# A two-layer encoder on one core: the opening's gate product, the order behind it, and the first strip of an up projection

## The chip, the core and the metric

The kernel runs on one core of a Trainium2 chip. The metric is the device time of one execution in microseconds (us), the median of three runs. The core has a matrix engine (TensorE, PE in the rows; its weight loads are PEld), a vector engine (VectorE, DVE), ScalarE (ACT), GpSimd (POOL) and SyncE (SP), which run side by side and wait for one another on semaphores. Matrix products go to eight banks of PSUM, 512 float32 wide; everything else lies in SBUF.

## The reference

The input is 1024 tokens of 1024 numbers. Layer 0 mixes them with 8 stick-breaking and 8 forgetting heads of 64, layer 1 with 16 heads over a shared latent and a top-k choice of keys; each layer ends in a gated feed-forward block of width 2816 with a causal convolution. What matters here, cut from it:

```python
h = x @ w_in                                   # layer 0: q, k, v of 16 heads, and 8 gate columns
f_logit = parts[6] + b_f
cum = jnp.cumsum(jax.nn.log_sigmoid(f_logit.astype(F32)), axis=1)
logits = (q @ k) * scale + cq[..., None] - cum_k[:, :, None, :]     # forgetting heads
w = exp(log_sigmoid(z) + after)                # stick-breaking heads
x = layer_norm(ALPHA * x + mixer(x))
gate, up = jnp.split(x @ w_up, 2, axis=-1)
x = layer_norm(ALPHA * x + (gelu(conv(gate)) * up) @ w_down)
```

## The kernel before

**Numbers in two parts.** Every float32 operand is split into a high and a low bfloat16 part (`_hi`, `_lo`), and a product is three matmuls: high by high, high by low, low by high. A weight piece of 128x1024 is loaded by SP into one of four slots (`w_stage`), its high part is made by POOL or ScalarE (`w_hi`), its low part by POOL (`w_lo`), and a slot is free again when TensorE has used it (`w_used`).

**The opening** (`start_*`). The transposed input `xt_f` comes in eight tiles `k`; for each, ScalarE makes `xt_hi` and the vector engine `xt_lo`, and TensorE runs the gate product (8 columns of weights, both halves of the tokens, into banks 0 and 1: line 475) and two halves of pair 0's projection of q (`proj_half`, line 573). Then ScalarE computes the log-sigmoid of the gate in four steps (lines 431 to 437), the vector engine scans it into a cumulative sum (`gate_c`, line 501) and writes it as three bfloat16 parts into `cum_rows` (lines 504 to 507, three rounds). The forgetting heads alone need these, and they come after the four stick-breaking pairs.

**The heads** (`heads_*`). TensorE goes on with halves 2 to 5 of pair 0's projection (k, then v: lines 573 and 579). ScalarE copies each half out of PSUM as a high part (`proj_evac_hi`, line 619), the vector engine the low part (`proj_evac_lo`, line 624), and ScalarE issues the DMAs that lay q and k (`make_current_qk`, six for each head of the pair, line 636) and v (`make_current_v`, two each, line 644) as the scores need them, and three that store `cum_rows` (line 1041). Then `all_pairs` runs eight pairs of heads, 16 slots each: a slot has the scores of one block of queries on TensorE (lines 745 and 748), for stick-breaking two sigmoids on ScalarE (`stay`, `take`, lines 832 and 834), a scan on the vector engine (line 881) and a product on POOL (line 902). The next pair's projection is run in between, into bank 4; `half_slots` says which part in which slot. `heads_gpsimd` splits the pieces of the next pair (lines 890 and 895), each when its use in the projection is over.

**The end of a mixer** (`back_and_norm`, tags `o0` and `o1`; the same function, with 22 tiles in place of 8, ends the feed-forward blocks). The output projection runs in two groups of four blocks of 128 tokens, the late half of the tokens first (line 317). The vector engine adds the residual and normalizes; TensorE turns a normalized block with eight transposes (`turn`, line 1204); ScalarE writes its high parts and a float32 copy (`highs`, lines 1258 and 1260) and the vector engine its low parts (`lows`, line 1332). In between TensorE runs the first products of the up projection: `unit(n, h, ks)`, strip `n` over token half `h`, by `early_strips` and `product_part` (line 341), late half first. On ScalarE the order is written by hand: `deviation(i)` is the root of block i's variance, `piece_hi` the high part of a strip. On each engine the order of the code is the order of execution; an instruction that waits holds up all behind it on its engine.

## Time and profile before

| | |
|---|---|
| median of three runs | 2903.4 us (2902.46 to 2911.68) |
| the profiled execution | 2908.67 us, its span 2906.9 us |
| TensorE busy | 2803.3 us, 96% of the span |
| vector engine, POOL, ScalarE busy | 64%, 57%, 37% |
| mean granted clock of TensorE | 0.991 |

A row of a timeline is: start in us, duration in us, engine, line, operation, output<-inputs, how many; and in square brackets how long the engine stood idle before it, with what ended that. Matmuls overlap: the next starts before the row of the last is over. Lines with ACTq or SPq are the issuing of DMAs. The granted clock is the share of TensorE's full clock (2.4 GHz) that it was given in a stretch; it has two levels, full and half.

### The profile page before, as it was taken

What the parts mean: (1) busy time and instruction counts of PE and PEld (TensorE: products, weight loads), DVE (VectorE), ACT (ScalarE), POOL (GpSimd) and SP (SyncE); (2) the same over time, 40 slices, a digit from 0 to 9 for tenths busy, and PEclk for the clock granted to TensorE, in tenths of its full rate; (3) what the DMA queues carried; (4) which work ended last, traced back from release to release, by engine and by line L of the source; (5) the groups of instructions that cost most, each with busy time, mean ns of one, the idle gap of its engine ahead of it and who ended that gap; (6) DMA issues with size and microseconds to landing.
All of it is one profiled execution on the core that took longest, in us unless ns stands there. A gap on an engine that the chain in (4) does not pass through costs nothing.

```text
span 2906.9 us, 44833 instructions
## 1 busy us (share of the span) xinstructions
PE 2803.3 (96%) x16880; PEld 1457.2 (50%) x16880; DVE 1872.9 (64%) x2732; ACT 1081.6 (37%) x1765; POOL 1651.6 (57%) x915
## 2 busy tenths in 40 slices
PE   7999998899999999999899999999999999999998
PEld 3566665444444444444444444677764444444443
DVE  5787666475666664355999999677756656665042
ACT  3565555333333310013553333666653333332000
POOL 3677545426666669845348777500013466665884
PEclk9999999999999999999999999999999999999999
DMA  4122222431111144222213222211113211113322
GB/s 146 48 62 67 61 67 47 157 119 44 59 59 59 59 158 145 102 81 77 59 37 145 101 88 85 74 59 43 58 71 111 80 59 58 59 59 111 135 102 102
DMA packets 102990, 240.57 MB, mean 83 GB/s; under 512 B 42448, under 2 KB 42576, under 8 KB 102848
## 3 DMA queue, kind: packets, MB, share of 16 engines
q1 hardware_dynamic: 56352, 204.13, 19.6%
q10 hardware_dynamic: 46496, 34.48, 4.6%
q8 instruction: 97, 1.59, 0.2%
q14 instruction: 45, 0.37, 0.0%
HBM read 185.31 MB, written 31.51 MB: 75 GB/s over the span
## 4 chain that ended last, share of the span: by engine, by line
PE 86%; DVE 5%; ACT 3%; issue 2%; ACTq 1%; POOL 1%; DMA 0%; POOLq 0%; DVEq 0%
PE ps L1483 22%; PE ps L317 19%; PE ps L306 14%; PE ps L2290 6%; PE ps L573 5%; PE ps L341 4%; PE ps L2326 2%; PE ps L683 2%; PE ps L579 2%; PE ps L1810 2%; PE ps L768 2%; PE ps L745 2%; PE ps L1854 1%; PE ps L2305 1%; DVE pt_lo L704 1%
## 5 line engine op out<-in xcount | busy, mean ns | idle before, releaser
L262 POOL TENSOR_TENSOR w_hi<-w_stage,ones 128x1024 bf16<-128x1024 f32 (+1 forms) x115 | 235.0, 2044 | 138.1 <-PE ps L317 85.1
L265 POOL TENSOR_TENSOR w_lo<-w_stage,w_hi 128x1024 bf16<-128x1024 f32 (+1 forms) x115 | 262.7, 2284 | 9.0
L1300 DVE SCALAR_TENSOR_TENSOR x_res<-x_res,ps 128x1024 f32<-128x1024 f32 x32 | 39.0, 1218 | 338.4 <-PE ps L317 337.5
L317 PE MATMUL ps<-w_hi,hid_hi 128*128 128x512 bf16 x704 | 209.4, 379 | 0.8 <-POOL w_lo L265 0.8
L317 PE MATMUL ps<-w_lo,hid_hi 128*128 128x512 bf16 x704 | 209.4, 379 | 0.0
L317 PE MATMUL ps<-w_hi,hid_lo 128*128 128x512 bf16 x704 | 209.4, 379 | 0.0
L2290 PE MATMUL ps<-lat_hi,q_now 128*128 128x512 bf16 (+3 forms) x768 | 197.7, 326 | 0.0
L306 PE MATMUL ps<-xt_hi,w_hi 128*128 128x512 bf16 x608 | 181.8, 381 | 2.5 <-DVE score L1969 2.5
L306 PE MATMUL ps<-xt_hi,w_lo 128*128 128x512 bf16 x608 | 181.3, 380 | 0.0
L306 PE MATMUL ps<-xt_lo,w_hi 128*128 128x512 bf16 x608 | 181.3, 380 | 0.0
L279 POOL TENSOR_TENSOR w_lo<-w_stage,w_hi 128x1024 bf16<-128x1024 f32 x32 | 76.6, 2399 | 155.4 <-ACT w_hi L272 155.2
L1483 PE MATMUL ps<-xt_hi,w_hi 128*128 128x512 bf16 x432 | 163.7, 379 | 0.0
L1483 PE MATMUL ps<-xt_lo,w_hi 128*128 128x512 bf16 x432 | 163.7, 379 | 0.0
L1483 PE MATMUL ps<-xt_hi,w_lo 128*128 128x512 bf16 x432 | 163.7, 379 | 0.0
L902 POOL TENSOR_TENSOR prob<-take,prob 128x1024 f32<-128x1024 f32 (+3 forms) x64 | 107.4, 1684 | 90.6 <-DVE prob L881 69.7
L2414 POOL COPY v_now_hi<-val_hi 128x512 bf16 (+1 forms) x16 | 9.8, 616 | 251.0 <-PE ps L2305 251.0
L1252 ACT ACTIVATE ln_rstd<-ln_rstd 128x1 f32<-128x1 f32 x32 | 6.5, 203 | 383.6 <-DVE ln_rstd L1312 383.5
L2205 DVE MATCH_REPLACE8 score<-best,score 128x512 f32<-128x512 f32 (+4 forms) x160 | 148.8, 943 | 0.0
L2202 DVE MAX8 best<-score 128x8 f32<-128x512 f32 (+4 forms) x160 | 140.5, 944 | 1.7
L1449 POOL TENSOR_TENSOR w_lo<-w_stage,w_hi 128x1024 bf16<-128x1024 f32 x36 | 76.7, 2130 | 113.5 <-ACT w_hi L1557 113.5
L2368 DVE CUSTOM_DVE_ANT_0 prob<-ps,hide 128x1024 f32<-128x1024 f32 (+7 forms) x128 | 96.5, 754 | 63.2 <-PE ps L2290 63.1
L704 DVE TENSOR_TENSOR pt_lo<-ps,pt_hi 128x512 bf16<-128x512 f32 x192 | 100.2, 549 | 51.7 <-ACT pt_hi L698 51.5
(293 smaller groups left out, 7896.9 us busy)
## 6 DMA issues: line engine op xcount, KB each, us to landing
w_stage<-in_l_up SPq DMA_DIRECT2D x88, 512.0 KB, 3.2
w_stage<-in_l_down SPq DMA_DIRECT2D x88, 512.0 KB, 3.2
w_stage<-in_l_o SPq DMA_DIRECT2D x32, 512.0 KB, 3.9
w_stage<-in_l_q SPq DMA_DIRECT2D x32, 512.0 KB, 4.8
q_split<-q_out SPq DMA_DIRECT2D x32, 512.0 KB, 2.6
q_now<-q_split SPq DMA_DIRECT2D x16, 1024.0 KB, 4.8
w_stage<-in_l_qkv SPq DMA_DIRECT2D x24, 512.0 KB, 3.3
x_spilled<-x_res ACTq DMA_DIRECT2D x16, 512.0 KB, 2.6
```

Source lines behind the costliest of these rows:

```text
L262: pool.tensor_tensor(w_hi[slot][:, 0:cols], w_stage[slot][:, 0:cols], ones[:, 0:1].to_broadcast([P, cols]), ALU.mult).then_inc(w_cast[slot ...
L265: pool.tensor_tensor(w_lo[slot][:, 0:cols], w_stage[slot][:, 0:cols], w_hi[slot][:, 0:cols], ALU.subtract).then_inc(w_split[slot], 1)
L306: mm = pe.matmul(ps[:, bank + h, :], w, a[:, k, h * HALF:(h + 1) * HALF], start=(first and k == k0 and m == 0), stop=(last and k == k1 - 1 ...
L317: mm = pe.matmul(ps[:, bank + h, :], a[:, k, rows], w[slot][:, h * HALF:(h + 1) * HALF], start=(k == 0 and m == 0), stop=(k == tiles - 1 a ...
L341: mm = pe.matmul(ps[:, bank + h, :], w, a[:, k, h * HALF:(h + 1) * HALF], start=(k == 0 and m == 0), stop=(k == KT - 1 and m == 2))
L573: mm = pe.matmul(ps[:, bank, :], w, a[:, u, h * HALF:(h + 1) * HALF], start=(u == 0 and m == 0), stop=(u == KT - 1 and m == 2))
L704: dve.tensor_tensor(lo, src, hi, ALU.subtract).then_inc(self.lo, 1)
L902: pool.tensor_tensor(prob[t % 4][:, 0:n], take[t % 4][:, 0:n], prob[t % 4][:, 0:n], ALU.mult).then_inc(s_wsb, 1)
L1483: mm = pe.matmul(ps[:, bank, :], wk[:, k * P:(k + 1) * P], ak[:, k, :], start=(k == 0 and q == 0), stop=(k == 3 and q == 2))
L2202: dve.max(best[:, c, :], cells[c]).then_inc(s_top, 1)
L2205: dve.match_replace(cells[c], best[:, c, :], cells[c], TAKEN_SCORE).then_inc(s_rep, 1)
L2290: mm = pe.matmul(ps[:, 2 * (t % 2) + c // 512, 0:w], a, b, start=(kt == 0 and m == 0), stop=(kt == 1 and m == 2))
```

## The change

It has four pieces. (1) The gate product: in place of three matmuls per half and `k` with 8 columns of weights there are two with 40 columns. `wf_both` holds the high part in columns 0 to 7 and the low part in columns 32 to 39, `wf_wide` the high part in columns 0 to 7 and zeros elsewhere. Rows 0 to 7 of PSUM then hold two of the three products and rows 32 to 39 the third; ScalarE takes rows 32 to 39 with the bias, and the vector engine adds rows 0 to 7 to them. (2) The order behind it, on the vector engine and ScalarE; the waits of TensorE for the gate and for all six halves of pair 0 go or become a wait for three. (3) In `back_and_norm` with eight tiles (`o0` and `o1`): ScalarE's `piece_hi` of strip 0 stands before `deviation(GROUP + 2)`. (4) There too: strip 0's unit over the early half is cut into 384 tokens, after the third block's low parts, and 128, after the fourth's.

```diff
-        def product_part(pe, feed, n, h, ks):
+        def product_part(pe, feed, n, h, ks, cols=slice(0, HALF)):
...
-                    mm = pe.matmul(ps[:, bank + h, :], w, a[:, k, h * HALF:(h + 1) * HALF],
+                    mm = pe.matmul(ps[:, bank + h, cols], w, a[:, k, h * HALF + cols.start:h * HALF + cols.stop],
...
-            act.activation(gate_x[:, :], banks(0)[0:8, :], ACT.Identity, bias=gate_b[:, 0:1]).then_inc(s_gact, 1)
-            act.wait_ge(s_gact, 1)
+            act.activation(gate_x[:, :], banks(0)[32:40, :], ACT.Identity, bias=gate_b[:, 0:1]).then_inc(s_gact, 1)
+            act.wait_ge(s_gdve, 1)
...
+            pool.memset(wf_both[:, :, :], 0.0).then_inc(s_wfh, 1)
+            pool.memset(wf_wide[:, :, :], 0.0).then_inc(s_wfh, 1)
+            pool.wait_ge(s_wfh, 2)
             pool.wait_ge(s_wf, 32)
-            pool.tensor_copy(wf_hi[:, :, :], wf_f[:, :, :]).then_inc(s_wfh, 1)
-            pool.wait_ge(s_wfh, 1)
-            pool.tensor_tensor(wf_lo[:, :, :], wf_f[:, :, :], wf_hi[:, :, :], ALU.subtract).then_inc(s_wfl, 1)
+            pool.tensor_copy(wf_both[:, :, 0:8], wf_f[:, :, :]).then_inc(s_wfh, 1)
+            pool.tensor_copy(wf_wide[:, :, 0:8], wf_f[:, :, :]).then_inc(s_wfl, 1)
+            pool.wait_ge(s_wfh, 3)
+            pool.tensor_tensor(wf_both[:, :, 32:40], wf_f[:, :, :], wf_both[:, :, 0:8], ALU.subtract).then_inc(s_wfl, 1)
...
-                    for m, (w, a) in enumerate(((wf_hi, xt_hi), (wf_hi, xt_lo), (wf_lo, xt_hi))):
-                        mm = pe.matmul(ps[0:8, h, :], w[:, k, :], a[:, k, h * HALF:(h + 1) * HALF],
+                    for m, (w, a) in enumerate(((wf_both, xt_hi), (wf_wide, xt_lo))):
+                        mm = pe.matmul(ps[0:40, h, :], w[:, k, :], a[:, k, h * HALF:(h + 1) * HALF],
...
+            gthen(dve.tensor_tensor(gate_x[:, :], banks(0)[0:8, :], gate_x[:, :], ALU.add))
...
-                    if not first:
+                    if isinstance(pair, int) and pair == 1 and e == 0:
+                        pe.wait_ge(s_pjl, 3)
+                    elif not first:
                         pe.wait_ge(s_pjl, 6 * pair + e)
...
+                if prev is None and slot == 8:
+                    act.wait_ge(s_gdve, GATE_STEPS)
+                    for r in range(3):
+                        act.dma_start(cum_dram[:, r, :], cum_rows[32 * r:32 * r + 8, :]).then_inc(s_cum, 16)
...
-            pe.wait_ge(s_gdve, GATE_STEPS)
...
-                pe.wait_ge(s_nl, 2 * TB * at + 2 * TB)
-                for n in range(4):
+                if tiles == KT:
+                    pe.wait_ge(s_nl, 2 * TB * at + 2 * (TB - 1))
+                    early(pe, 0, 0, range(KT), slice(0, HALF - P))
+                    pe.wait_ge(s_nl, 2 * TB * at + 2 * TB)
+                    early(pe, 0, 0, range(KT), slice(HALF - P, HALF))
+                else:
+                    pe.wait_ge(s_nl, 2 * TB * at + 2 * TB)
+                    unit(0, 0, range(KT))
+                for n in range(1, 4):
                     unit(n, 0, range(KT))
...
+                if tiles == KT:
+                    piece_hi(act, next_feed, 0)
                 deviation(GROUP + 2)
                 highs(3)
                 if tiles == KT:
-                    for n in range(SLOTS):
+                    for n in range(1, SLOTS):
```

What it does to the order is best seen engine by engine. The vector engine behind the opening's last `xt_lo`, before (`gate_*` is the gate, `nq`, `nk`, `nv` the parts of the projected pair):

```order
L499 TENSOR_SCALAR gate_m<-gate_x 8x1024
L501 SCALAR_TENSOR_TENSOR gate_c<-gate_m,gate_a 8x1024
L504 CAST gate_p<-gate_c 8x1024
L505 COPY cum_rows<-gate_p 8x1024
L507 TENSOR_TENSOR gate_c<-gate_c,gate_p 8x1024
L504 CAST gate_p<-gate_c 8x1024
L505 COPY cum_rows<-gate_p 8x1024
L507 TENSOR_TENSOR gate_c<-gate_c,gate_p 8x1024
L504 CAST gate_p<-gate_c 8x1024
L505 COPY cum_rows<-gate_p 8x1024
L624 TENSOR_TENSOR nq_lo<-ps,nq_hi 128x512 x2
L624 TENSOR_TENSOR nk_lo<-ps,nk_hi 128x512 x2
```

The same place in the changed kernel:

```order
L504 TENSOR_TENSOR gate_x<-ps,gate_x 8x1024
L505 TENSOR_SCALAR gate_m<-gate_x 8x1024
L507 SCALAR_TENSOR_TENSOR gate_c<-gate_m,gate_a 8x1024
L635 TENSOR_TENSOR nq_lo<-ps,nq_hi 128x512 x2
L512 CAST gate_p<-gate_c 8x1024
L513 COPY cum_rows<-gate_p 8x1024
L515 TENSOR_TENSOR gate_c<-gate_c,gate_p 8x1024
L635 TENSOR_TENSOR nk_lo<-ps,nk_hi 128x512
L512 CAST gate_p<-gate_c 8x1024
L513 COPY cum_rows<-gate_p 8x1024
L515 TENSOR_TENSOR gate_c<-gate_c,gate_p 8x1024
L635 TENSOR_TENSOR nk_lo<-ps,nk_hi 128x512
```

One addition is new at the front, the low parts of q and k stand between the gate's rounds, and the third round comes behind them. ScalarE from pair 0's last k half to its first score, before (the DMAs make the operands of the scores and store the gate):

```order
L619 ACTIVATE nk_hi<-ps 128x512 x2
L636 DMA q_both_101<-nq_hi 64x1024
L636 DMA q_both_101<-nq_lo 64x1024
L636 DMA k_twice_103<-nk_hi 64x1024 x2
L636 DMA q_ext_105<-nq_hi 64x1024
L636 DMA k_ext_107<-nk_lo 64x1024
L636 DMA q_both_102<-nq_hi 64x1024
L636 DMA q_both_102<-nq_lo 64x1024
L636 DMA k_twice_104<-nk_hi 64x1024 x2
L636 DMA q_ext_106<-nq_hi 64x1024
L636 DMA k_ext_108<-nk_lo 64x1024
L619 ACTIVATE nv_hi<-ps 128x512 x2
```

The same place in the changed kernel:

```order
L630 ACTIVATE nk_hi<-ps 128x512 x2
L647 DMA q_both_101<-nq_hi 64x1024
L647 DMA q_both_101<-nq_lo 64x1024
L647 DMA k_twice_103<-nk_hi 64x1024 x2
L647 DMA q_ext_105<-nq_hi 64x1024
L647 DMA k_ext_107<-nk_lo 64x1024
L630 ACTIVATE nv_hi<-ps 128x512 x2
L647 DMA q_both_102<-nq_hi 64x1024
L647 DMA q_both_102<-nq_lo 64x1024
L647 DMA k_twice_104<-nk_hi 64x1024 x2
L647 DMA q_ext_106<-nq_hi 64x1024
L647 DMA k_ext_108<-nk_lo 64x1024
```

The copies of v have moved ahead of the second head's six DMAs. In both kernels v's four DMAs follow; before, the three of `cum_rows` stood behind those and ahead of the first `stay`, and now they stand in slot 8. ScalarE in `o0`, around the third block of the late half being turned, before (`w_hi_66` to `w_hi_69` are the strips of the up projection in slots 0 to 3):

```order
L1263 DMA x_spilled<-x_res 128x1024
L1252 ACTIVATE ln_rstd<-ln_rstd 128x1
L1258 ACTIVATE xt_hi<-ps 128x4x128
L1260 ACTIVATE xt_f_130<-ps 128x4x128
L1258 ACTIVATE xt_hi<-ps 128x4x128
L1260 ACTIVATE xt_f_130<-ps 128x4x128
L1263 DMA x_spilled<-x_res 128x1024
L272 ACTIVATE w_hi_66<-w_stage_62 128x1024
L272 ACTIVATE w_hi_67<-w_stage_63 128x1024
L272 ACTIVATE w_hi_68<-w_stage_64 128x1024
L272 ACTIVATE w_hi_69<-w_stage_65 128x1024
```

The same place in the changed kernel:

```order
L1281 DMA x_spilled<-x_res 128x1024
L272 ACTIVATE w_hi_66<-w_stage_62 128x1024
L1270 ACTIVATE ln_rstd<-ln_rstd 128x1
L1276 ACTIVATE xt_hi<-ps 128x4x128
L1278 ACTIVATE xt_f_130<-ps 128x4x128
L1276 ACTIVATE xt_hi<-ps 128x4x128
L1278 ACTIVATE xt_f_130<-ps 128x4x128
L1281 DMA x_spilled<-x_res 128x1024
L272 ACTIVATE w_hi_67<-w_stage_63 128x1024
L272 ACTIVATE w_hi_68<-w_stage_64 128x1024
L272 ACTIVATE w_hi_69<-w_stage_65 128x1024
```

Strip 0's high part has moved ahead of a block's deviation and of its four copies.

## Rows read from the trace of the kernel before

**Rows 1.** Waits of TensorE in the whole span: us in total, times, longest us.

```profile
PE ps L683 <- DVE pt_lo L704: 35.2, 31, 2.5
...
PE ps L341 <- DVE xt_lo L1332: 7.9, 3, 3.0
PE ps L341 <- POOL w_lo L279: 7.4, 2, 3.7
```

**Rows 2.** Timeline of TensorE, the opening's first gate block.

```profile
9.48 0.63 PE L475 MATMUL ps<-xt_lo,wf_hi 128*8 128x512 bf16 x1
```

**Rows 3.** Timeline of POOL, 4 to 50 us.

```profile
4.96 0.24 POOL L462 CAST wf_hi<-wf_f 128x64 bf16<-128x64 f32 x1 [2.27 <-DMA gate_b<-in_l_bf]
...
47.43 2.46 POOL L895 TENSOR_TENSOR w_lo<-w_stage,w_hi 128x1024 bf16<-128x1024 f32 x1
```

**Rows 4.** Timeline of the vector engine, 37 to 50 us.

```profile
37.32 3.44 DVE L501 TENSOR_TENSOR_SCAN gate_c<-gate_m,gate_a 8x1024 f32<-8x1024 f32 x1 [2.66 <-ACT gate_a L437]
...
43.21 0.68 DVE L504 CAST gate_p<-gate_c 8x1024 bf16<-8x1024 f32 x1
...
47.92 2.24 DVE L505 COPY cum_rows<-gate_p 8x1024 bf16<-8x1024 bf16 x1
```

**Rows 5.** Timeline of ScalarE, from the gate to the first score.

```profile
32.84 1.11 ACT L431 ACTIVATE gate_x<-ps,gate_b 8x1024 f32<-8x1024 f32 x1 [13.91 <-PE ps L475]
...
52.77 0.54 ACTq L636 DMA_DIRECT2D q_both<-nq_hi  x1
...
60.51 1.09 ACT L619 ACTIVATE nv_hi<-ps 128x512 bf16<-128x512 f32 x2 [15.31 <-issue]
62.46 0.69 ACTq L644 DMA_DIRECT2D v_both<-nv_hi  x1
...
65.93 1.29 ACTq L1041 DMA_DIRECT2D cum_rows<-cum_rows  x3
67.26 1.02 ACT L832 ACTIVATE stay<-ps 128x1024 f32<-128x1024 f32 x1 [5.66 <-issue]
```

**Rows 6.** Timeline of TensorE, pair 0's first scores.

```profile
58.45 0.38 PE L745 MATMUL ps<-k_twice,q_both 128*128 128x512 bf16 x1 [3.16 <-DMA k_ext<-nk_lo]
```

**Rows 7.** Timeline of ScalarE, end of layer 0's mixer.

```profile
618.67 0.20 ACT L1252 ACTIVATE ln_rstd<-ln_rstd 128x1 f32<-128x1 f32 x1 [3.71 <-DVE ln_rstd L1312]
...
620.69 3.91 ACT L272 ACTIVATE w_hi<-w_stage 128x1024 bf16<-128x1024 f32 x4
```

**Rows 8.** Timeline of TensorE, end of layer 0's mixer.

```profile
608.09 1.06 PE L1204 MATMUL ps<-ident,x_res 128*128 128x128 f32 x8 [0.45 <-DVE xt_lo L1332]
...
624.94 0.38 PE L341 MATMUL ps<-xt_hi,w_hi 128*128 128x512 bf16 x1 [3.68 <-POOL w_lo L279]
...
653.95 0.61 PE L341 MATMUL ps<-xt_hi,w_hi 128*128 128x512 bf16 x1 [2.95 <-DVE xt_lo L1332]
```

**Rows 9.** Timeline of POOL, end of layer 0's mixer.

```profile
621.93 11.08 POOL L279 TENSOR_TENSOR w_lo<-w_stage,w_hi 128x1024 bf16<-128x1024 f32 x4 [21.96 <-ACT w_hi L272]
```

**Rows 10.** Timeline of the vector engine, end of layer 0's mixer.

```profile
620.92 0.69 DVE L1332 TENSOR_TENSOR xt_lo<-ps,xt_hi 128x512 bf16<-128x512 f32 x1 [0.28 <-ACT xt_f L1260]
...
649.54 1.28 DVE L1332 TENSOR_TENSOR xt_lo<-ps,xt_hi 128x512 bf16<-128x512 f32 x2
...
653.20 0.69 DVE L1332 TENSOR_TENSOR xt_lo<-ps,xt_hi 128x512 bf16<-128x512 f32 x1 [0.29 <-ACT xt_f L1260]
```

**Rows 11.** Stretches of TensorE: us, busy us (count), granted clock, DMA share, GB/s.

```profile
624.90:630.00 5.10, 5.06 (x16) 0.67 0.48 162
653.90:661.00 7.10, 7.05 (x19) 0.57 0.00 0
2278.50:2285.00 6.50, 6.45 (x24) 0.79 0.00 0
690.00:1060.00 370.00, 370.00 (x1716) 1.00 0.19 66
44.40:55.20 10.80, 10.80 (x193) 1.00 0.25 74
```

33 lines of the change are left out of this document (17 added, 16 removed).

## Prediction

> **What bounds the kernel now.** I read the waits of TensorE first, because the table above has it busy for 96% of the span: a change can only pay where TensorE stands still or runs slowly on the way. Two of the longer waits belong to the lines of this change: line 341 (the first units of an up projection) waits 7.4 us in two places for POOL's `w_lo`, and 7.9 us in three places for the vector engine's `xt_lo` [rows 1]. The third of these three is behind layer 0's down projection, where `tiles` is not `KT` and nothing changes. Then the opening's timelines, engine by engine, for the chain that leads to the first pair of heads. Last the stretches after the waits, for the granted clock, and 690 to 1060 us, where the up projection keeps TensorE busy without a gap at full clock [rows 11]: time won ahead of it can arrive there undiminished.
>
> **Part A, the opening.** *Matmuls.* A matmul of 512 columns takes 0.216 us of TensorE's time at full clock (370 us for 1716 of them [rows 11]; the 0.38 us of a row overlap). The change drops a third of the gate's 48 matmuls: two per `k`. From `k` = 1 on that is 7 x 2 x 0.216 = 3.0 us. The two of `k` = 0 ran at half rate (0.63 us in the row, overlapping again [rows 2]); what they save, 0.9 us at most, is partly spent in waiting for the first `w_lo`: I take 0.4. So the gate product ends at 29.4 instead of 32.8 us and the last projection of pair 0 at 51.8 instead of 55.2. POOL's two new memsets and one copy are costed at nothing: POOL waits 2.27 us for the gate's weights there, and its cast of them takes 0.24 us [rows 3], so that the memsets fit into the wait; uncovered, the three would cost under 1 us.
>
> *Gate chain.* ScalarE's `gate_x` starts at 32.84 [rows 5], now 29.45. The new addition on the vector engine (8x1024, two operands) has no row of its own; it is bounded by the cast (0.68 us) and by the scan (3.44) [rows 4]. I take 1.25, what the subtraction leaves of a gate round of 2.45 us, since it is the nearest in form. The scan then starts at 35.2 instead of 37.32 and ends at 38.6 at the latest. Then come two `nq_lo` (0.65 each: four such fill the time from 50.16, the copy's end, to 52.7), a round of cast, copy and subtraction (40.76 to 43.21: 2.45 us [rows 4]), and one `nk_lo`: 43.0. The next cast and copy fall on POOL's split of pair 1's second piece, which waits for the fourth projection half: its second step moves by 3.4 us from 47.43 to 44.0 [rows 3] and ends at about 46.1. Before, the copy beside that step needed 2.24 us [rows 4]; so it ends at about 46.3, the subtraction at 47.5, `nk_lo` at T1 = 48.1 us. Before, T1 was 52.7: the DMAs behind it start at 52.77 [rows 5].
>
> What the rows show: the copy that started at 47.92 ended 0.27 us behind POOL's step [rows 3, 4]. The Trainium skill, "SBUF — State Buffer", § Who interferes with whom, says that such a vector copy and a POOL operation lock each other out, and that whoever issues first keeps the ports for the whole instruction; the trace agrees. By that rule the copy could also come first, and T1 would be 45.5.
>
> *ScalarE to the first score.* Six DMAs take half of 7.74 us (52.77 to 60.51), 3.87; the four of `v` 3.47 (62.46 to 65.93); the `cum_rows` three 1.33 [rows 5]. Now: 48.1 + 3.87 = 52.0, two `nv_hi` 1.1 (TensorE is done at 51.8), six DMAs to 56.9, four to 60.4, and `stay` of slot 0 at 60.45 instead of 67.26: 6.8 us. With T1 = 45.5 TensorE's 51.8 binds and it is 7.4. TensorE itself started slot 0 1.9 us behind the sixth DMA issue (56.6), at 58.45 [rows 6], now at 54, and fits two projection parts in ahead of ScalarE. Removing its waits for the gate and for pair 0's `nv_lo` costs nothing and frees nothing more, since ScalarE then comes last. The `cum_rows` DMAs stand in ScalarE's slot 8 now: 1.33 us ahead of `stay`, with turned blocks queued behind it, whose `pt_hi` the vector engine and then TensorE wait for. Between nothing and 1.3 us I take 0.3, since TensorE has projections to run there. Part A: 6.5 us, with ends 4.5 and 7.5.
>
> **Part B, the first high part earlier (both layers).** ScalarE makes the four `w_hi` from 620.69 on; POOL starts the first `w_lo` 1.24 us later, at 621.93 (four in 11.08 us), and TensorE starts the unit at 624.94 [rows 7 to 9], having ended the output projection about 621.2 (the wait is 3.68). In the new order the first `w_hi` stands ahead of `deviation`, for which ScalarE waits until 618.67 [rows 7]. Its slot is free when TensorE has done the first of the last block's four products of six matmuls, 3 x 6 x 0.216 = 3.9 us before the end: 617.4. So `w_hi` runs from 617.4 to 618.5, still ahead of 618.67: the moved step is paid from idle time, and would cost 0.2 us for each 0.2 us that it came later. POOL starts at 618.7 and ends at 621.5 at the latest. Next late is `xt_lo` of the fourth block, 620.92 + 0.69 = 621.61 [rows 10], and TensorE starts at 621.67: 3.27 us sooner. The other three `w_lo` keep their times (621.9 on) and are 2 us ahead of TensorE's units of 5.2 us. The residue is a gap of 0.4 us; at 608.09 one of 0.45 us left no slow matmul behind it [rows 8].
>
> The clock comes on top. In 624.90 to 630.00 the mean grant is 0.67, 2.4 and 1.2 GHz mixed: (1 - 0.67) x 5.1 = 1.7 us are lost behind the wait of 3.68 us [rows 11]. Layer 1 has the same wait (two of 7.4 us together [rows 1]) and is taken alike. Part B: 2 x (3.27 + 1.7) = 9.9 us, 6.5 without the clock.
>
> **Part C, 384 tokens and then 128 (both layers).** TensorE stands 2.95 us before 653.95, until `xt_lo` of the last block (653.20 + 0.69) [rows 8, 10]. The first 384 tokens need only the block before: its two `xt_lo` end at 650.8 [rows 10], when TensorE ends the last turning (651.0). So the gap closes: 2.93 us. The 24 matmuls become 48. Of 128 columns, 193 took 10.80 us, 0.056 each, with their weight loads [rows 11]; 384 columns by interpolation to 0.216 are 0.163, an estimate. 24 x (0.163 + 0.056) = 5.25 against 24 x 0.216 = 5.18: 0.1 us more. The first part lasts 3.9 us, to 654.9, and the last block is ready at 653.9. Clock: (1 - 0.57) x 7.1 = 3.05 us in layer 0, (1 - 0.79) x 6.5 = 1.4 in layer 1 [rows 11]. Part C: 5.9 + 4.2 = 10.1 us, 5.7 without the clock. The up projection's next pieces are split once their slot's unit is done, so they move with TensorE; the token sums move with `xt_lo`, 6 us less, but TensorE reads them only two tile pairs (some 40 us) later.
>
> **Sum.** 6.5 + 9.9 + 10.1 = 26.5 us: the span goes from 2906.9 to 2880.4. The profiled execution lies 5.3 us above the median of the runs shown; against the median, 2903.4 - 26.5 = 2876.9.
>
> **Rivals.**
> 1. *The clock doesn't come back.* The engine stays slow for such stretches at these places, because turning and copying phases, not the two gaps, bring it down. Against: the slow stretches begin just behind the gaps. The gain is 26.5 - 7.8 = 18.7: 2884.7.
> 2. *The opening's gain is spent among the pairs.* TensorE waits 35.2 us in 31 places for `pt_lo` there [rows 1]; `cum_rows` at slot 8 and a slower first pair take it back: 20 us gained or somewhat less, 2883.
> 3. *Part B stays shut.* If the slot is released later than 617.4, or the `w_hi` delays `deviation` and the fourth block, each us of that takes a us, and the clock falls as before: without part B, 16.6 us, 2886.8.
> 4. *Slower.* The copy beside POOL took 2.24 us, 1.97 of it before POOL's step ended [rows 3, 4]. The four stick-breaking pairs have 64 scans, and a new phase between the vector engine and POOL could block more of them. From 14 more such waits on the path the 26.5 us are gone; 18 cost 35 us: 2912. Against: what starts the pairs moves as one, so the phase hardly changes.
> 5. *It doesn't do what it says.* If another semaphore held line 341 in both places, parts B and C give nothing: 2897. The waits' releasers speak against it.
>
> **How the numbers follow.** Forecast 0.66 (2872 to 2881), rival 1 0.10, rival 2 0.13, rival 3 0.06, rival 4 0.02, rival 5 0.03. The range goes down to 2869 (part A at 7.5, layer 1's clock loss at layer 0's size, 1.7 us more, and the scatter of the runs, some 5 us) and up to 2887 for rivals 1 to 3. A difference under 0.3% (8.7 us) is no change that a measurement of this kernel can tell: faster takes the forecast, rivals 1 to 3, and the rest lies in rivals 4 and 5: 0.95, 0.03 and 0.02.
>
> **What would show it.** In the changed kernel's trace: `gate_x` on ScalarE near 29.5 us; the first `stay` near 60.5 and not above 62; in both layers the `w_hi` of slot 0 in ScalarE's idle time and line 341 starting within 0.5 us of the output projection's end; no wait between the last turning and the 384-column matmuls; no stretch at half rate behind either. I am wrong if these stand and the span has moved by less than 20 us (the time is given back in the pairs or behind 690 us), or if a slow stretch appears with no gap ahead of it.

## The result, and the profile of the changed kernel

The changed kernel takes 2884.3 us (median of 7 runs, 2882.7 to 2889.3); seven runs of the kernel before on the same chip have a median of 2911.6 us (2902.5 to 2915.1). The ratio is 0.9921, with a 95% interval of 0.9911 to 0.9931: 23 us less, between 20 and 26. (The two medians differ by 27.2 us, the two means by 23.7; the seven runs of before scatter over 13 us, so I go by the ratio.) A second comparison (e5 below) gave 0.9932 (0.9915 to 0.9949). The forecast was 26.5 us less, just outside the first interval, and 2884.3 us lies above the forecast's own band (2872 to 2881) and inside the wider range that goes up to 2887. The profiled execution took 2884.34 us, its span is 2882.5 (24.4 less), and its mean granted clock is 0.995 in place of 0.991.

I compare the two traces by checkpoints: the same line's start in both. The difference is what has been won up to there in this one pair of traces; in single traces the gain at the end of layer 0's mixer scatters by some us (8.9 is the largest of nine profiles with part A, see below).

| checkpoint | won, us | forecast, us |
|---|---|---|
| first `stay` | 8.6 | 6.8 |
| pair 0, slot 8 (line 768) | 10.3 | |
| layer 0, first root of a variance (line 1252) | 8.9 | 6.5 |
| layer 0, behind the slow stretch after part B's gap | 13.85 | 11.5 |
| layer 0, first `conv` (behind part C) | 19.8 | 17.4 |
| layer 1, index stage, first product of line 1810 | 19.6 | |
| layer 1, index stage, last product of line 1810 | 15.4 | |
| layer 1, last turning ahead of part C | 20.0 | |
| the end | 24.4 | 26.5 |

In this pair of traces parts A, B and C all gave what was forecast or more; 4.2 us are missing in a stage of layer 1 that the prediction did not name. The waits of TensorE in the changed kernel (us in total, times, longest) show both. They answer to [rows 1], where `w_lo` of line 341 stood with 7.4 us and `xt_lo` with 7.9; of the 3.6 us left here, 2.4 belong to a third place, behind layer 0's down projection, and the qi wait was 2.3 us before:

```profile
PE ps L694 <- DVE pt_lo L715: 33.9, 29, 2.5
...
PE ps L1830 <- DVE qi L1996: 4.7, 1, 4.7
PE ps L694 <- POOL prob L936: 3.9, 3, 2.1
PE ps L341 <- DVE xt_lo L1352: 3.6, 3, 2.4
```

**The opening.** Timeline of the vector engine in the changed kernel, from the new addition on; it answers to [rows 4]. The addition took 1.21 us (taken at 1.25), the scan 2.29 and not 3.44:

```profile
29.65 1.21 DVE L504 TENSOR_TENSOR gate_x<-ps,gate_x 8x1024 f32<-8x1024 f32 x1 [6.91 <-ACT gate_x L431]
30.89 1.48 DVE L505 TENSOR_SCALAR gate_m<-gate_x 8x1024 f32<-8x1024 f32 x1
34.23 2.29 DVE L507 TENSOR_TENSOR_SCAN gate_c<-gate_m,gate_a 8x1024 f32<-8x1024 f32 x1 [1.85 <-ACT gate_a L437]
...
40.76 1.98 DVE L512 CAST gate_p<-gate_c 8x1024 bf16<-8x1024 f32 x1
42.77 2.24 DVE L513 COPY cum_rows<-gate_p 8x1024 bf16<-8x1024 bf16 x1
```

POOL at the same time, answering to [rows 3]: the copy started 0.50 us behind POOL's second step and ended 0.28 us behind its end, as it did before.

```profile
42.27 2.46 POOL L910 TENSOR_TENSOR w_lo<-w_stage,w_hi 128x1024 bf16<-128x1024 f32 x1
```

ScalarE, answering to [rows 5]: the gate, the first DMA behind the fourth low part, the first of the four for v, and the first score.

```profile
28.43 1.11 ACT L431 ACTIVATE gate_x<-ps,gate_b 8x1024 f32<-8x1024 f32 x1 [9.30 <-PE ps L479]
...
47.07 0.55 ACTq L647 DMA_DIRECT2D q_both<-nq_hi  x1
...
54.81 0.69 ACTq L655 DMA_DIRECT2D v_both<-nv_hi  x1
...
58.68 1.02 ACT L847 ACTIVATE stay<-ps 128x1024 f32<-128x1024 f32 x1 [6.68 <-issue]
```

From `gate_x` to the DMA there are 18.64 us, where the prediction's sum has 18.65 (48.1 - 29.45). From there to `stay` there are 11.6 us, where it has 12.35.

**The end of layer 0's mixer.** Part B, answering to [rows 7 to 10]: ScalarE makes strip 0's `w_hi` after 2.51 us of idling, in which it waited for the slot, and the root follows 0.14 us later; POOL's `w_lo` starts at 609.78; the last `xt_lo` of the late half ends at 612.69; TensorE starts 0.06 us behind it, after a gap of 0.41 us in place of 3.68. In layer 1 the gap left is 0.77 us (at 2231.21), a little more than the 0.5 us that the prediction allowed.

```profile
608.55 1.06 ACT L272 ACTIVATE w_hi<-w_stage 128x1024 bf16<-128x1024 f32 x1 [2.51 <-PE ps L317]
609.75 0.20 ACT L1270 ACTIVATE ln_rstd<-ln_rstd 128x1 f32<-128x1 f32 x1
```

```profile
609.78 2.13 POOL L279 TENSOR_TENSOR w_lo<-w_stage,w_hi 128x1024 bf16<-128x1024 f32 x1 [18.71 <-ACT w_hi L272]
```

```profile
612.00 0.69 DVE L1352 TENSOR_TENSOR xt_lo<-ps,xt_hi 128x512 bf16<-128x512 f32 x1 [0.28 <-ACT xt_f L1278]
```

```profile
612.75 0.39 PE L341 MATMUL ps<-xt_hi,w_hi 128*128 128x512 bf16 x1 [0.41 <-DVE xt_lo L1352]
```

Part C: the 384 columns start while the last turning's row still runs, with no idle time in brackets. They follow each other in 0.16 us (taken at 0.163) from the second on, those of 128 columns in 0.056 us.

```profile
636.10 1.04 PE L1215 MATMUL ps<-ident,x_res 128*128 128x128 f32 x8
637.02 0.34 PE L341 MATMUL ps<-xt_hi,w_hi 128*128 128x384 bf16 x1
637.20 0.33 PE L341 MATMUL ps<-xt_lo,w_hi 128*128 128x384 bf16 x1
```

TensorE in the stretches behind part B's place, part C's place in layer 0 and part C's place in layer 1 (us, busy us of PE, PEld, DVE, ACT and POOL with counts, granted clock, DMA share, GB/s). They answer to the first three rows of [rows 11], which had 0.67, 0.57 and 0.79:

```profile
612.70:617.80 5.10, 4.99 (x23) 2.34 (x25) 4.99 (x4) 2.04 (x3) 4.79 (x2) 1.00 0.41 141
637.00:644.00 7.00, 6.95 (x58) 4.49 (x57) 5.07 (x5) 3.80 (x5) 1.69 (x1) 1.00 0.20 77
2254.00:2262.00 8.00, 7.95 (x65) 5.34 (x65) 6.07 (x7) 3.58 (x6) 1.23 (x1) 1.00 0.20 81
```

**Where 4.2 us went.** In layer 1's index stage ScalarE copies a strip by four DMAs; POOL multiplies the result, the vector engine adds it, and at the end TensorE waits for `qi`. The kernel before: ScalarE's issues, SP's next load of weights (512 KB), and POOL.

```profile
1312.76 2.55 ACTq L1887 DMA_DIRECT2D strip_w<-strip_f  x4
```

```profile
1316.22 0.32 SPq L241 DMA_DIRECT2D w_stage<-in_l_qidx  x1
```

```profile
1317.29 2.35 POOL L1828 TENSOR_TENSOR strip_w<-strip_w,rope_i_sin 128x1024 f32<-128x1024 f32 x1 [1.09 <-DMA strip_w<-strip_f]
```

The changed kernel:

```profile
1292.94 3.69 ACTq L1907 DMA_DIRECT2D strip_w<-strip_f  x4
```

```profile
1296.12 0.32 SPq L241 DMA_DIRECT2D w_stage<-in_l_qidx  x1
```

```profile
1300.66 2.36 POOL L1848 TENSOR_TENSOR strip_w<-strip_w,rope_i_sin 128x1024 f32<-128x1024 f32 x1 [4.56 <-DMA strip_w<-strip_f]
```

The first issue is at 1312.76 and at 1292.94. The four take 2.55 us before and 3.69 in the changed kernel: the fourth took 1.75 us in place of 0.61. SP's load, which was issued 0.9 us behind the last copy before, is now issued 0.5 us ahead of that issue's end. POOL starts 7.7 us behind the first issue in place of 4.5, and TensorE's wait for `qi` is 4.7 us in place of 2.3. Of the 4.2 us this wait makes 2.4; half-rate stretches behind it cost 1.2 us, where the kernel before had none in this stage. Beside the copies lies a transfer of a queue that carries instructions (row of the DMA queues from 1294.5 to 1295.0 us: packets, MB, share):

```profile
q8 instruction: 1, 0.02, 17.6%
```

### The profile page after: what moved, and what is told of

Same layout as the page of the kernel before. It is cut to its first block, busy times and chain, and to the rows that moved or that the text cites. A ratio compares the mean times of both kernels' runs of the same rounds, so it can differ in the third digit from the quotient of the medians.

```text
span 2882.5 us, 44624 instructions
## 1 busy us (share of the span) xinstructions
PE 2773.1 (96%) x16630; PEld 1456.3 (51%) x16912; DVE 1876.8 (65%) x2733; ACT 1081.0 (38%) x1765; POOL 1653.8 (57%) x918
## 3 DMA queue, kind: packets, MB, share of 16 engines
q1 hardware_dynamic: 56352, 204.13, 19.9%
## 4 chain that ended last, share of the span: by engine, by line
PE 85%; DVE 4%; ACT 3%; issue 3%; POOL 2%; ACTq 1%; DMA 0%; POOLq 0%; DVEq 0%
PE ps L1503 23%; PE ps L317 20%; PE ps L306 13%; PE ps L2310 6%; PE ps L584 5%; PE ps L341 3%; PE ps L2346 2%; PE ps L590 2%; PE ps L694 2%; PE ps L1830 2%; PE ps L779 2%; PE ps L756 2%; PE ps L2325 1%; PE ps L1874 1%; DVE pt_lo L715 1%
## 5 line engine op out<-in xcount | busy, mean ns | idle before, releaser
L2310 PE MATMUL ps<-lat_hi,q_now 128*128 128x512 bf16 (+3 forms) x730 | 185.9, 323 | 1.2
L306 PE MATMUL ps<-xt_hi,w_hi 128*128 128x512 bf16 x598 | 179.2, 380 | 3.1 <-DVE score L1989 2.5
L306 PE MATMUL ps<-xt_hi,w_lo 128*128 128x512 bf16 x596 | 178.6, 380 | 0.8 <-issue 0.2
L1503 PE MATMUL ps<-xt_hi,w_hi 128*128 128x512 bf16 x422 | 159.9, 379 | 0.5
L1503 PE MATMUL ps<-xt_hi,w_lo 128*128 128x512 bf16 x422 | 159.9, 379 | 0.3
L936 POOL TENSOR_TENSOR prob<-prob,row_inv 128x1024 f32<-128x1024 f32 (+3 forms) x64 | 73.3, 1148 | 105.7 <-DVE row_inv L891 105.6
```

The costliest lines, as they stand in the source:

```text
L306: mm = pe.matmul(ps[:, bank + h, :], w, a[:, k, h * HALF:(h + 1) * HALF], start=(first and k == k0 and m == 0), stop=(last and k == k1 - 1 ...
L1503: mm = pe.matmul(ps[:, bank, :], wk[:, k * P:(k + 1) * P], ak[:, k, :], start=(k == 0 and q == 0), stop=(k == 3 and q == 2))
L2310: mm = pe.matmul(ps[:, 2 * (t % 2) + c // 512, 0:w], a, b, start=(kt == 0 and m == 0), stop=(kt == 1 and m == 2))
```

## Experiments

Beside each timed ratio (to the kernel before on the same chip) I read in each trace the checkpoints and the granted clock in steps of 2 us. A half-rate stretch's loss is (1 - clock) times busy time, summed over neighbouring steps under 0.97.

### Parts A, B and C apart (e1, e2, e8, e11)

Each kernel is the kernel before with the hunks of the diff of that part and no others. e1 has part A; e2 has B and C; e8 has B:

```diff
+                if tiles == KT:
+                    piece_hi(act, next_feed, 0)
                 deviation(GROUP + 2)
...
-                    for n in range(SLOTS):
+                    for n in range(1, SLOTS):
```

and e11 has C: the `cols` argument and

```diff
+                    pe.wait_ge(s_nl, 2 * TB * at + 2 * (TB - 1))
+                    early(pe, 0, 0, range(KT), slice(0, HALF - P))
+                    pe.wait_ge(s_nl, 2 * TB * at + 2 * TB)
+                    early(pe, 0, 0, range(KT), slice(HALF - P, HALF))
```

> The kernel before with part A alone (gate product with 40 columns, new order behind it, the stores of cum_rows in slot 8); parts B and C are undone. Theory 1 (the three parts are independent and add up): the first stay starts 8.6 us sooner than before, the stick-breaking pairs run 10.3 us sooner, the end of layer 0's mixer 8.9 us, and nothing more is won; the time is 9 us less (ratio 0.997), and 4 us more of it may be lost in layer 1's index stage if the slow DMA issue of the changed kernel (1.75 us in place of 0.61) turns up here too. Rival (the opening's gain is given back behind the pairs, and what the changed kernel has at 600 us comes from elsewhere): under 5 us, ratio above 0.998.

> The kernel before with parts B and C (first high part ahead of a block's deviation; 384 tokens and then 128), and without part A. Theory 1 (additive): 4.9 + 6.0 us in layer 0 and 4.7 + 4.3 us in layer 1, 19.9 us together: ratio 0.9931; 4 us less if layer 1's index stage loses what it lost in the changed kernel. Rival (parts B and C profit from part A's shift): 15 us or less in the two places together. For the index stage, theory 2 (the loss is a slow DMA issue by ScalarE, a thing of the single run) gives a qi wait of 2.3 us as before in this run; its rival (every shift of the phase brings it) gives 4.7 us here too.

> The kernel before with part B alone (the first high part ahead of a block's deviation, in both layers). Theory 3: the gap of 3.68 us becomes 0.4 us and no half-rate stretch follows: 3.27 us and 1.3 to 1.7 us in each layer, 9 to 10 us together, of which the part C gap behind it may take some back through the clock: ratio 0.9966. In the trace the half-rate stretches near 621 and 2245 us are gone and those behind part C's place (650 and 2275 us) appear in some executions and not in others, 0 to 3.9 us each. Rival (B's gap only moves to the next wait): the turnings behind the first units wait longer and under 5 us are gained.

> The kernel before with part C alone (384 tokens and then 128, in both layers). Theory 3: the gap of 2.95 us is gone in both layers and no half-rate stretch follows at its place; the stretches of 1.3 to 1.7 us behind part B's gap of 3.68 us stay. 5.9 us for the gaps, and 0 to 4.4 us for the clock, since in the profiles so far with this gap open 0, 1.7, 1.7 and 3.0 us were lost behind it in layer 0, and 0, 1.4, 1.5 and 1.6 us in layer 1: 8.6 us on the mean, ratio 0.997. Rival (part C needs part B, because POOL's low parts of the further strips come late without it): waits of line 341 for POOL's w_lo take 1 us and more ahead of strips 1 to 3 of the early half.

| kernel | median, us | ratio, 95% interval | us less |
|---|---|---|---|
| e1, A | 2900.3 | 0.9972 (0.9962 to 0.9982) | 8 |
| e8, B | 2900.6 | 0.9972 (0.9963 to 0.9982) | 8 |
| e11, C | 2903.5 | 0.9977 (0.9968 to 0.9986) | 7 |
| e2, B and C | 2892.2 | 0.9947 (0.9931 to 0.9964) | 15 |
| changed, A, B and C | 2884.3 | 0.9921 (0.9911 to 0.9931) | 23 |

The parts add up: 8 + 8 + 7 = 23, and B and C together are 15. Theory 1 stands as far as the times can tell: each of the three has an interval of about 3 us to either side, so that the sum could miss some us, and the loss in the index stage, which none of e1, e2, e8 and e11 has, does not show in it. In single traces they add up less neatly: e1's `stay` was 7.4 us sooner, but only 4.0 were left at the end of the stick-breaking pairs (10.3 expected), and 4.1 at the end of the mixer. e2 was expected at 0.9931, the edge of its interval, and gave some 5 us less, which may be the clock terms: 19.9 was read against one profile of before. Its `qi` wait was 2.2 us, as theory 2 had it. In e8 and e11 the gaps closed as expected (0.41 us; none), and no wait for `w_lo` of 1 us came up in e11.

### The clock behind the gaps (e3, e4)

e3 throws matmuls into the gaps of the kernel before, so that the gaps' time stays lost and TensorE is busy in them:

```diff
                     pe.wait_ge(s_acc, TB * at + GROUP + 1 + bank_of.index(2 * n))
+                    if n == 0 and tiles == KT:
+                        for _ in range(14):
+                            pe.matmul(ps[:, 1, :], xt_hi[:, 0, HALF:HALF + P], xt_hi[:, 0, HALF:SEQ],
+                                      start=True, stop=True)
...
                 turn(GROUP + 3)
+                if tiles == KT:
+                    pe.wait_ge(s_nl, 2 * TB * at + 2 * (TB - 1))
+                    for _ in range(17):
+                        pe.matmul(ps[:, 0, 0:HALF - P], xt_hi[:, 0, 0:P], xt_hi[:, 0, 0:HALF - P],
+                                  start=True, stop=True)
```

> The kernel before, with work thrown into two of TensorE's gaps in each layer: 14 matmuls of 512 columns ahead of the wait for the up projection's first weights (part B's gap of 3.68 us), 17 of 384 columns ahead of the wait for the last block's low parts (part C's gap of 2.95 us). Their results are overwritten; nothing else is changed, so the gaps' own time stays lost. Theory 3 (the half-rate stretches behind come from the gaps alone): granted clock 1.00 in both stretches of both layers and 1.7 + 3.05 us less in layer 0, 1.7 + 1.4 us in layer 1, 7.8 us together, ratio 0.9973. Rival (turning and copying phases bring the clock down and not the gaps): the clock stays at 0.57 to 0.8 behind them and the time within 1 us of before.

It took 2902.0 us, ratio 0.9981 (0.9971 to 0.9990): 5.5 us less (3 to 8) with 62 matmuls more, where the rival had no gain. The same stretches as in the first two of [rows 11] are at full clock (columns as above):

```profile
627.05:632.15 5.10, 5.10 (x25) 2.37 (x25) 5.00 (x7) 0.20 (x1) 5.10 (x3) 1.00 0.50 152
656.10:663.20 7.10, 7.10 (x34) 3.23 (x33) 3.78 (x4) 4.25 (x3) 6.59 (x2) 1.00 0.00 0
```

e4 opens part C's gap again in the changed kernel and keeps its cut:

```diff
-                    pe.wait_ge(s_nl, 2 * TB * at + 2 * (TB - 1))
-                    early(pe, 0, 0, range(KT), slice(0, HALF - P))
                     pe.wait_ge(s_nl, 2 * TB * at + 2 * TB)
+                    early(pe, 0, 0, range(KT), slice(0, HALF - P))
```

> The changed kernel, with the wait for the last block's low parts ahead of both pieces of strip 0's unit: the cut into 384 and 128 columns stays, and part C's gap of 2.95 us opens again in both layers. Theory 3: the stretch behind it runs slow again, and all of part C is gone in both layers: 6.0 + 4.3 = 10.3 us more than the changed kernel, of which 5.9 us are the gaps and the rest the clock, ratio to before near 0.9957. Rival (the gain comes from smaller matmuls or from elsewhere, not from the wait): within 3 us of the changed kernel, 0.992.

It took 2899.0 us, ratio 0.9968 (0.9956 to 0.9981), some 13 us more than the changed kernel; forecast were 10.3, within the width of the intervals. The gap is back at 2.95 us in both layers, and slow matmuls behind it:

```profile
644.30:651.30 7.00, 6.93 (x49) 4.25 (x49) 2.21 (x2) 1.91 (x1) 4.51 (x1) 0.76 0.01 2
2270.30:2277.30 7.00, 6.98 (x49) 4.33 (x50) 2.16 (x1) 1.91 (x1) 4.53 (x1) 0.76 0.01 2
```

But the same gap has not the same price in each execution. In e1 it is open too, at 2.95 us, and the stretch behind it ran at full clock, while the one behind part B's gap did not:

```profile
620.80:625.90 5.10, 5.02 (x16) 1.99 (x17) 5.00 (x7) 0.20 (x1) 5.10 (x3) 0.67 0.49 153
649.80:656.80 7.00, 6.91 (x32) 3.15 (x33) 3.71 (x4) 3.35 (x3) 4.69 (x2) 1.00 0.01 2
```

Lost behind the gaps, in us, in the profiles in which they are open (e14 is the kernel before but for 8 matmuls elsewhere); where a gap is closed or filled, no profile shows a loss:

| profile | B, layer 0 | B, layer 1 | C, layer 0 | C, layer 1 |
|---|---|---|---|---|
| before | 1.7 | 1.7 | 3.0 | 1.4 |
| e1 | 1.6 | 1.3 | 0 | 0 |
| e11 | 1.7 | 1.5 | closed | closed |
| e8 | closed | closed | 1.7 | 1.5 |
| e4 | closed | closed | 1.7 | 1.6 |
| e14 | 1.6 | 1.3 | 0 | 0 |
| mean | 1.65 | 1.45 | 1.3 | 0.9 |

The means sum to 5.3 us, near e3's 5.5; the prediction had 7.8. Theory 3 stands for the cause. That its amount was too large rests on these profiles: e3's time (3 to 8 us) does not exclude 7.8.

### The opening's two halves (e9, e10), and the stores (e15)

e9 is the changed kernel with the three matmuls of 8 columns again, and without the addition; e10 has the new product and the order of before behind it, the stores of `cum_rows` ahead of the first `stay` and TensorE's old waits included (cut from it):

```diff
-            for e in range(2):
-                proj_evac_lo(dve, e, 0)
...
-                    proj_evac_lo(dve, 2 + r, 0)
...
-            make_current_qk(act, 0, 0)
+            for hh in range(2):
+                make_current_qk(act, hh, 0)
             for e in range(4, 6):
                 proj_evac_hi(act, e, 0)
-            make_current_qk(act, 1, 0)
```

e15 moves the stores of `cum_rows`:

```diff
-                if prev is None and slot == 8:
+                if prev is None and slot == 0:
```

> The changed kernel with the gate product of before (three matmuls of 8 columns for each half and k, no addition on the vector engine), in the new order. Theory 1: the product's own share of the first stay is what the gate product ends sooner by, 3.4 to 4.4 us, less the new addition's 1.2; but the first k halves, which stand behind the gate product on TensorE, move back whole. The first stay at 58.7 + 3.4 = 62.1 us or somewhat sooner, and 3 us more than the changed kernel, ratio 0.9935. Rival (the product pays nothing, since the vector engine's chain decides): the first stay within 1 us of 58.7.

> The changed kernel with the order of before behind the gate product (the gate's three rounds ahead of all low parts of q and k, the copies of v behind the second head's DMAs, the stores of cum_rows ahead of the first stay), with the new product. Theory 1: the order's share is the rest, 7.7 - 3.4 = 4.3 us: the first stay at 63 us, and 4 us more than the changed kernel, ratio 0.994. Rival (the order alone makes the whole gain, since it takes the vector engine's gate rounds off the path): the first stay at 66 to 67 us.

> The changed kernel with the three stores of cum_rows in ScalarE's slot 0 of the first pair, ahead of the first stay, in place of slot 8. Theory 1 (as the prediction has it: 1.33 us on the path at slot 0, 0.3 us at slot 8): the first stay 1.3 us later, at 60.0 us, and 1 us at the end. Rival (the first pair has slack of its own, or the stores at slot 8 hold up as much): no difference in the stick-breaking pairs' end.

e9 took 2889.9 us, ratio 0.9935 (0.9921 to 0.9948), with the first `stay` at 62.38; e10 took 2892.9 us, 0.9945 (0.9932 to 0.9959), with it at 65.11; e15 took 2891.7 us, 0.9938 (0.9923 to 0.9952), with it at 61.24. In the nine profiles that have part A whole, `stay` starts 6.9 to 8.6 us sooner than at 67.26, 7.8 on the mean, and in the five others without any of it within 1.0 us of 67.26. So the product alone is worth 2.2 us there, the order alone 4.9, both 7.8. For e10, 63 was expected: the order is worth more and the product less than I split them. The stores at slot 0 cost 1.8 us at the first `stay` against the mean of the nine (1.3 expected), or 1.1 if both are counted from the start of `gate_x`. In the time, e15 and e5 (0.9938 and 0.9932) can't be told apart.

The gain at the first `stay` is not yet a gain behind the pairs. At the end of layer 0's mixer, against the mean of the six profiles without part A, the nine with all of it stand 7.7 us better, but e9 1.4, e10 2.1 and e15 2.5. These three are single profiles, in a place where those of equal code differ by up to 5.9 us, so this is a hint and no more. e9's ratio hit its forecast of 0.9935, but partly by luck: it has no slow issue in the index stage, and beside the kernels with all three parts that have none either (e6, e13 and e16, 0.9912 to 0.9916) it is some 6 us slower and not 3, with an interval of 4 us to either side.

### What differs between executions (e5), and the slow issue (e7, e12, e13, e14)

e5 is the changed kernel once more. e7 holds SP's load back until the copies have landed, and e12 shifts ScalarE's code:

```diff
             load_first(sp, feed_qidx)
+            sp.wait_ge(s_sw5[0], 64)
             load_rest(sp, feed_qidx)
```

```diff
+            for _ in range(40):
+                act.wait_ge(s_const, CONST_STEPS)
             copy_strip(0, 0, 0, 2, small_used(0), 0, 0)
```

> The changed kernel once more, unchanged, beside the kernel before on one chip. Theory 4 (where the granted clock falls, and whether one of ScalarE's DMA issues in the index stage takes 1 to 2 us in place of 0.61, differs from one execution to the next of the same kernel): the profile shows another set of half-rate stretches than the first profile of this kernel, whose sum was 8.9 us, among 4 and 14 us, and a qi wait of either 2.3 us or 4.7 us; the first stay again within 1 us of 58.7. Rival (they are fixed by the code): the same stretches within 0.3 us, and the slow issue again. Ratio to before 0.992 by both.

> The changed kernel, with SP's first load of the second round of index weights held until the first strip's four copies have landed. In two of six profiles so far (the changed kernel and the one with both waits) one of ScalarE's copies was issued slowly, the 512 KB load went ahead of the last copy, which then landed 5.6 us after its issue in place of 2.3 to 3.8, and TensorE's wait for qi was 4.7 and 4.9 us in place of 2.3. Theory 6 (the load in front makes most of it): the copies land within 4 us of their issue and the qi wait is 2.3 to 3.4 us whether or not an issue is slow; up to 2 us less than the changed kernel. Rival (the slow issue alone does it, or the held load becomes late itself): 4.7 us if an issue is slow, no gain or a loss.

> The changed kernel with 40 waits that are long satisfied in ScalarE's idle time ahead of the index stage's first copy, so that the code from there on lies 40 instructions further. In the four profiles with a slow DMA issue one transfer of the queue for instructions took place 1.2 to 1.8 us behind the first copy's issue and beside the copies' data; in the six without it the transfer came ahead of the copies or behind them. Theory 7 (ScalarE waits for its own program there): the transfer moves ahead of the copies, no issue takes over 0.63 us, and the qi wait is 2.3 us: 2 to 4 us less than the changed kernel. Rival (the transfer is another engine's or plays no part): the fourth issue takes 1.7 to 2.0 us as before, the qi wait is 4.7 to 4.9 us.

e5 took 2889.2 us, 0.9932 (0.9915 to 0.9949). Its profile lost 10.9 us to half-rate stretches (8.9 in the first), partly in other places: theory 4 stands for the clock. But the slow issue was there again, 1.80 us with a `qi` wait of 4.9, and so it was in e4, e7, e12 and e15: it is no chance, and there theory 4 falls. e7 took 2886.1 us, 0.9928 (0.9911 to 0.9944). The issue was slow (1.75), the last copy landed 4.3 us behind its issue at most, and the wait was 3.3 us: the load in front makes 1.4 to 1.6 of the 2.5 us by which the wait grows, the issue the rest. (e14 below has a slow issue with no load in front, and a wait of 3.1 us.) e12 took 2888.5 us, 0.9931 (0.9916 to 0.9946); an issue took 1.49 us and the wait was 4.8: theory 7 falls, the code is not ScalarE's.

In every profile with a slow issue a transfer of the queue for instructions lies beside the copies. Its place against the first copy's issue follows the number of TensorE's matmuls ahead of it in the program (steps of 0.5 us, the step's start is given):

| profiles | matmuls against before | transfer, us behind first issue | slowest issue, us | `qi` wait, us |
|---|---|---|---|---|
| e1 | -16 | 7.3 | 0.63 | 2.3 |
| before, e8 | 0 | 3.7, 3.5 | 0.63 | 2.3, 2.2 |
| changed, e4, e5, e7, e12, e15 | +8 | 1.5 to 1.8 | 1.49 to 2.08 | 4.7 to 5.0 (e7 3.3) |
| e10 | +8 | 2.0 | 0.63 | 3.2 |
| e2, e9, e11 | +24 | -1.6 to -2.0 | 0.6 | 2.2 to 2.3 |
| e3 | +31 | -3.7 | 0.63 | 2.2 |

(e13 and e14 are told below; e6 and e16, +32 matmuls and one wait less, have the transfer at -1.3. In e10 the transfer comes at the end of the issues, which stay quick, and POOL waits 2.8 us. In e2, e9, e10 and e11 one issue of 0.9 to 1.1 us occurs at a later strip.) So theory 8: part A takes 16 matmuls out of the opening and part C puts 24 into layer 0, and the sum moves the loading of TensorE's own program onto ScalarE's copies, some 650 us further on. (That the queue is TensorE's is inferred from its place, which goes with the number of TensorE's matmuls.) e13 and e14 test it from both sides, with small matmuls in a wait of 2 us behind layer 0's down projection:

```diff
                 turn(GROUP + 3)
+                if tiles != KT:
+                    pe.wait_ge(s_nl, 2 * TB * at + 2 * (TB - 1))
+                    for _ in range(24):
+                        pe.matmul(ps[:, 0, 0:16], xt_hi[:, 0, 0:P], xt_hi[:, 0, 0:16],
+                                  start=True, stop=True)
```

(24 of them in the changed kernel, 8 in the kernel before.)

> The changed kernel with 24 matmuls of 16 columns thrown into TensorE's wait of 2.0 to 2.4 us behind layer 0's down projection; their results are overwritten. Theory 8 (the transfer of the instruction queue near 1294 us is TensorE's program; its place against the copies follows the number of TensorE's matmuls ahead of it): over the profiles the transfer stood 3.7 us behind the first copy's issue in the kernel before, 7.3 with part A alone (16 matmuls less), -2.0 with part C alone (24 more), 1.5 to 2.0 with both. 24 more matmuls bring it from 1.6 to 2 us or more ahead of the copies: no issue over 0.7 us, the qi wait 2.3 us, and 2 to 4 us less than the changed kernel. Rival (chance, or ScalarE's own doing): an issue of 1.5 to 2.0 us and a wait of 4.7 to 4.9 us, as in four of five profiles with parts A, B or C together and this code.

> The kernel before with 8 such matmuls of 16 columns in the same wait. Theory 8: the transfer moves from 3.7 us behind the first copy's issue to about 2.0 us (8 matmuls with their weight loads are 1.7 us of TensorE's program at 0.216 us each), where it stood in the changed kernel; an issue takes 0.95 to 2.0 us and TensorE's wait for qi is 3.2 to 4.9 us in place of 2.3: 1 to 4 us more than before, ratio 1.0003 to 1.0015. Rival: 0.61 us, 2.3 us and 1.000, as in all profiles of kernels near this one so far.

e13 took 2884.4 us, ratio 0.9916 (0.9903 to 0.9928). The transfer came 3.7 us ahead of the copies (the queue's row of that half us: packets, MB, share):

```profile
q8 instruction: 1, 0.02, 14.1%
```

and ScalarE's issues, POOL's wait and TensorE's are as in the kernel before:

```profile
1295.74 2.55 ACTq L1912 DMA_DIRECT2D strip_w<-strip_f  x4
```

```profile
1300.13 2.35 POOL L1853 TENSOR_TENSOR strip_w<-strip_w,rope_i_sin 128x1024 f32<-128x1024 f32 x1 [1.24 <-DMA strip_w<-strip_f]
```

```profile
PE ps L1835 <- DVE qi L2001: 2.2, 1, 2.2
```

Its span is 2879.4 us. Of what had been won up to the first `conv` (17.1 us) 0.2 were lost in the index stage, where the changed kernel lost 4.4 and e5 6.7. The time agrees with that but does not show it by itself: 0.9916 against 0.9921 and 0.9932 is 1 to 5 us less, with intervals of 3 us and more to either side.

e14 took 2909.9 us, ratio 1.0008 (1.0000 to 1.0017). 8 small matmuls, which take 0.41 us in a wait of 2 us, brought the slow issue into the kernel before:

```profile
1315.76 3.62 ACTq L1892 DMA_DIRECT2D strip_w<-strip_f  x4
```

```profile
PE ps L1815 <- DVE qi L1981: 3.1, 1, 3.1
```

The transfer was 1.7 us behind the first issue (about 2.0 expected), an issue took 1.69 us, and the wait 3.1, just under the 3.2 expected. Its size in time (2 us, between 0 and 5) is at the edge of what can be measured, and not all of it need be the index stage: the half-rate stretch at the third place cost 3.8 us in this profile and 2.3 before. The Trainium skill, "Runtime: NRT & Kernel Launch", § Instruction fetch mechanics, says that an engine's instructions come in blocks of 16 KiB over a DMA queue and that this is mostly hidden. The rows agree with the size (0.02 MB, rounded) and, for TensorE, with the second: no wait of TensorE stands at the transfer. e14 shows that it need not be hidden for the others. Theory 8 stands: the profiles show the place of the transfer and its effect both ways. An issue is slow in the seven profiles in which the transfer starts 1.5 to 1.8 us behind the first issue, and in none of the other eleven. That the transfer delays the issue by holding its queue or the DMA engines is argued, not shown.

### The third place (e6, e16)

```diff
-                if tiles == KT:
-                    pe.wait_ge(s_nl, 2 * TB * at + 2 * (TB - 1))
...
-                else:
-                    pe.wait_ge(s_nl, 2 * TB * at + 2 * TB)
-                    unit(0, 0, range(KT))
+                pe.wait_ge(s_nl, 2 * TB * at + 2 * (TB - 1))
+                early(pe, 0, 0, range(KT), slice(0, HALF - P))
+                pe.wait_ge(s_nl, 2 * TB * at + 2 * TB)
+                early(pe, 0, 0, range(KT), slice(HALF - P, HALF))
```

> The changed kernel, with the 384 and 128 cut in the third place too: behind layer 0's down projection, where strip 0 of the index stage's weights is multiplied. There TensorE waits 2.0 to 2.4 us for the last block's low parts, and 2.2 to 2.9 us were lost to the half clock behind it in every profile so far. Theory 5 (part C's mechanism carries over): the wait of 2.0 to 2.4 us is gone, and the half-rate stretch too if the gap brought it: 2 to 4.7 us less than the changed kernel. Rival (TensorE has stood still 1.4 us ahead of the last turning as well, so that the clock falls anyway): 2 us, with the slow stretch still there.

> The changed kernel with the cut of 384 and 128 in the third place too, once more, with more rounds. Theories 5 and 8 together: the wait of 2.0 us is gone, and the 24 matmuls more keep the transfer ahead of the copies, so that the qi wait is 2.3 us again: 4 to 7 us less than the changed kernel, ratio to before 0.990 to 0.9915. Rival (the first profile had luck in the index stage): an issue over 1.4 us and a qi wait of 4.7 us, 2 to 3 us less than the changed kernel.

The two gave 2881.2 us, 0.9912 (0.9896 to 0.9929), and 2883.6 us, 0.9913 (0.9900 to 0.9925). The wait is gone and 2.3 to 2.6 us are won across it in both traces. A half-rate stretch stays, though: 1.6 and 1.7 us lost, in place of 2.1 to 2.9 in the others (3.8 in e14). TensorE stands still for 1.35 us ahead of the last turning there as well, and that gap is open:

```profile
1282.51 1.09 PE L1215 MATMUL ps<-ident,x_res 128*128 128x128 f32 x8 [1.35 <-DVE x_res L1340]
```

```profile
1283.70:1290.70 7.00, 6.99 (x49) 4.32 (x50) 1.29 (x2) 1.02 (x2) 0.00 (x0) 0.77 0.00 0
```

So the rival of e6 was right on the clock. The transfer came 1.3 us ahead of the copies, no issue took over 0.63 us, and the `qi` wait was 2.2 us in both. e16 and e13 ran on the same chip and differ by 0.7 us, less than can be told: a good part of this version's gain over the changed kernel may be the 24 matmuls moving the transfer, and the 2.3 to 2.6 us at the third place show in the traces alone. It has the lowest ratio, some 4 us less than the changed kernel's if both comparisons of each are taken together, which is about the width of the intervals.

## Why the prediction came out as it did

**Part A, forecast 6.5 us.** 7.8 us at the first `stay` and, over the nine profiles with part A and the six without, 7.7 at the end of layer 0's mixer (5.5 against -2.1 us); e1's time gives 8, within 5 to 11. The chain from `gate_x` to the first DMA was right to 0.01 us, and that is luck: the scan took 2.29 us and not 3.44, but the second cast then fell on POOL's first step and took 1.98 us and not 0.68. What held was the mechanism, that the copy ends with POOL's second step. The copy took 2.24 us beside POOL again, as the row said; T1 = 45.5, by the rule from the Trainium skill, "SBUF — State Buffer", § Who interferes with whom, did not come about, since the copy again started behind POOL's step. Under-sized were two things: the gate product ended 0.4 us sooner on the mean (`gate_x` at 28.4 to 29.9, mean 29.1, forecast 29.45), and the two `nv_hi`, 1.1 us, cost nothing on ScalarE's chain, because the DMAs' issues went on beside them.

**Part B, forecast 3.27 us and 1.7 per layer.** 4.93 us in layer 0 and 4.6 to 4.9 in layer 1. `w_hi` was made before the root was due, and what came next was `xt_lo`, with a gap of 0.41 us (0.77 in layer 1).

**Part C, forecast 2.93 us and 3.05 or 1.4.** 5.97 and 4.3 us against this one profile of before. The lengths of the parts were right. The clock term was mis-sized as an expectation: 3.05 was the largest of five values (0, 0, 1.7, 1.7, 3.0), read from one execution. Over all four places 5.3 us and not 7.8 were to be had on the mean of the profiles: 2.5 us too much.

**The step that failed** is what the sum put at nothing: everything behind the stages that it names. The first paragraph says that time won "can arrive there undiminished", and the sum carries this on to the end. From 690 to 1060 us it did. But the up projection was the last stretch that I looked at, and near 1293 us the number of TensorE's instructions, which no term of the sum had, put a program load beside another engine's copies, and TensorE waited 4.7 us for `qi` in place of 2.3. In the five profiles with such a wait (4.7 to 5.0 us: changed, e4, e5, e12, e15) 6.0 us on the mean are lost from the first `conv` to the last product of line 1810, in eight without a slow issue (before, e1, e2, e3, e8, e9, e11, e13) 1.8: 4.2 us. Of these, 2.6 are the wait itself. The rest is for the most part half-rate stretches in the stage, 2.6 us on the mean of the five and 1.2 of the eight; they come up without a slow issue too (3.2 us in e11), so that this part is not shown to be the load's. e7 and e14, which have the slow issue but waits of 3.3 and 3.1 us, lost 1.7 and 2.3 us.

The second step, smaller, is the clock term: right in its cause and 2.5 us too large. The sum becomes 26.5 + 1.3 (part A) - 2.5 (clock) - 4.2 (index stage; 2.6 if only the wait is taken) = 21.1 us, or 22.7, where the two comparisons gave 23 (20 to 26) and 20 (15 to 25).

**Rivals.** The measured time is near the 2884.7 and 2883 of rivals 1 and 2, but by neither's mechanism: the clock came back at all four places, and the opening's gain arrived. Rival 2 has a grain of truth in the single traces: up to the end of layer 0's mixer, where their code is the same, the traces with part A differ by up to 5.9 us and those without by 4.4, through half-rate stretches and the phase among the pairs. Rivals 3, 4 and 5 did not occur; part B's gap is 0.4 to 0.8 us in every kernel that has the part, and the other three `w_lo` were in time.

## What to carry to other kernels

Close the gap of an engine whose clock falls when it idles, and count the clock behind it too, but take its price from several executions. Split a unit by the data that comes last, where the first part covers the wait. After adding or removing instructions, compare the program loads (the instruction queues' rows) with short chains of DMAs far behind the change: 8 matmuls more moved a load onto one. And a single profile is too little for a chain of this length: the same code gave 3.1 to 8.9 us at the end of layer 0's mixer.

## What the runs showed of the hardware

- Half rate behind a gap of the same length (2.95 us, at the same place) cost 0 to 3.0 us in five executions; behind one of 3.7 to 4.0 us it cost 1.3 to 1.7 us in all eight cases, and behind those of 0.4 to 0.8 us nothing in any profile. The sum of all half-rate stretches ranges over 7.0 to 18.9 us among the profiles.
- A load of TensorE's program (by inference) moved against the copies by about 0.2 to 0.3 us for each matmul added ahead of it (0.12 in e6 and e16, where a wait of 2 us went too), and a ScalarE DMA issue beside it took 1.5 to 2.1 us in place of 0.61.
- A gap filled with useless matmuls was worth 5.5 us (3 to 8) in all: the kernel with 62 matmuls more was the faster one.
- ScalarE's activations and its DMA issues ran beside each other: `nv_hi` at 50.91 and 51.41, 0.6 us each, and issues at 51.02 and 51.55.
